# The steady phase of a decoder step: its blocks written out on four engines in place of a register loop

## What is computed

```python
def peer_ffn(x, w_q, sub_keys, peer_u, peer_v):
    q = (xt @ w_q).astype(jnp.float32).reshape(T, PEER_HEADS, 2, HALF)
    sc = jnp.einsum('thpd,hpnd->thpn', q, sub_keys.astype(jnp.float32))
    s_top, i_top = lax.top_k(sc, PEER_TOPK)
...
    def block(args):
        xc, ic, gc = args
        hu = jnp.einsum('tkd,td->tk', peer_u[ic], xc)
        act = jax.nn.gelu(hu, approximate=False) * gc
        return jnp.einsum('tk,tkd->td', act, peer_v[ic])

def decoder_layer(h, shift_prev, conv_buf, wkv, lp):
...
    h1 = layer_norm(ALPHA * h + mix, ln1_g, ln1_b)
    h2 = layer_norm(ALPHA * h1 + peer_ffn(h1, w_q, sub_keys, peer_u, peer_v), ln2_g, ln2_b)
```

## Time and profile before

| | |
|---|---|
| time, median of 3 runs | 3707.61 us (3704.52 to 3711.28) |
| the profiled execution's own time | 3712.13 us |
| its span, first to last instruction | 3710.4 us |
| PE busy with matmuls | 3241.3 us (87%) |
| DVE busy | 2429.9 us (65%) |
| POOL busy | 2110.3 us (57%) |
| ACT busy | 807.3 us (22%) |
| mean granted TensorE clock | 0.954 |
| moved by DMA | 1239.76 MB, 334 GB/s over the span |

### The profile page before, as it was taken

The page is one execution under the profiler, slowest core; times in us unless marked ns, Lnnn a source line. Parts: engine busy times, 40 slices in busy tenths (PEclk is TensorE's granted clock), DMA queues, the critical chain, the costliest instruction groups (busy, mean ns, idle before and its releaser), DMA issues.

```text
span 3710.4 us, 58003 instructions
## 1 busy us (share of the span) xinstructions
PE 3241.3 (87%) x17619; PEld 1712.6 (46%) x17619; DVE 2429.9 (65%) x5758; ACT 807.3 (22%) x1954; POOL 2110.3 (57%) x2172
## 2 busy tenths in 40 slices
PE   4996898599988998899889988998898899989877
PEld 3663565444544454445444544454445444533422
DVE  5463523757766776677667766776667767777695
ACT  2331001122222222222222222222222222222121
POOL 0012700466666666666666666666566666676575
PEclk9997999799999999999999999999999999999999
DMA  4344212899999999999999999999999999999997
GB/s 158 96 124 120 89 32 66 290 351 371 408 404 361 377 409 408 374 376 408 409 370 368 408 409 361 376 408 408 367 371 407 408 389 390 408 408 409 391 380 296
DMA packets 395689, 1239.76 MB, mean 334 GB/s; under 512 B 50834, under 2 KB 98326, under 8 KB 395216
## 3 DMA queue, kind: packets, MB, share of 16 engines
q0 software_dynamic: 302112, 1099.09, 76.6%
q1 hardware_dynamic: 91504, 134.41, 10.3%
q10 hardware_dynamic: 1728, 2.16, 0.2%
HBM read 1212.00 MB, written 31.94 MB: 335 GB/s over the span
## 4 chain that ended last, share of the span: by engine, by line
PE 53%; DMA 18%; DVE 10%; issue 7%; ACT 2%; POOL 2%; DVEq 0%; SPq 0%; ACTq 0%; POOLq 0%
PE ep_ps L1271 32%; DMA rings<-in_peer_v_dram,idx 15%; PE front_ps L1141 8%; PE ep_ps L1319 5%; PE front_ps L1193 3%; PE front_ps L1211 3%; DVE rings L1666 3%; DMA rings<-in_peer_u_dram,idx 2%; POOL rings L584 2%; ACT L1420 1%; ACT diag L1393 0%; DVE rings L1780 0%; PE front_ps L1202 0%; PE front_ps L1287 0%; PE front_ps L1220 0%
## 5 line engine op out<-in xcount | busy, mean ns | idle before, releaser
L1271 PE MATMUL ep_ps<-rings,diag 128*128 128x512 f32 x4096 | 2034.4, 625 | 288.4 <-ACT diag L1393 156.7
L584 POOL DMA_INDIRECT rings<-in_peer_u_dram,idx x1024 | 980.6, 958 | 777.2 <-issue 248.3
L1666 DVE CUSTOM_DVE_ANT_0 rings<-rings,x_ps 128x1024 f32<-128x1024 f32 x1024 | 1238.3, 1212 | 137.9 <-DMA rings<-in_peer_u_dram,idx 105.1
L584 POOL DMA_INDIRECT rings<-in_peer_v_dram,idx x1024 | 993.0, 970 | 470.6 <-issue 264.7
L1271 PEld LDWEIGHTS ep_ps<-rings,diag 128*128 128x128 f32 x4096 | 731.6, 195 | 1075.1 <-issue 772.5
L1393 ACT ACTIVATE diag<-ident,act_v 128x128 f32<-128x128 f32 x1024 | 347.7, 391 | 237.4 <-PE ep_ps L1271 141.6
L1211 PEld LDWEIGHTS front_ps<-h1T,wq_ring 128*128 128x128 f32 x2304 | 290.4, 199 | 63.5 <-issue 63.5
L1211 PE MATMUL front_ps<-h1T,wq_ring 128*128 128x128 f32 (+1 forms) x2304 | 290.7, 279 | 1.2 <-issue 1.2
L348 PE MATMUL job_ps<-rings,w_ring 128*128 128x352 f32 (+2 forms) x672 | 208.6, 473 | 7.7 <-ACTq L390 3.9
L1319 PE MATMUL ep_ps<-rings 128*128 128x352 f32 x576 | 197.1, 482 | 16.8 <-DVEq L1790 15.4
L1380 ACT ACTIVATE q_T<-front_ps 128x128 f32<-128x128 f32 (+1 forms) x144 | 38.5, 267 | 780.3 <-PE front_ps L1211 780.3
(11 more groups left out here) (349 smaller groups left out, 2877.5 us busy)
## 6 DMA issues: line engine op xcount, KB each, us to landing
wq_ring<-scratch_wq_tiles SPq DMA_DIRECT2D x144, 512.0 KB, 7.5
rings<-in_peer_u_dram,idx POOLq DMA_INDIRECT x1024, 13.7
rings<-in_peer_v_dram,idx POOLq DMA_INDIRECT x1024, 13.1
ops<-scratch_op_blocks SPq DMA_DIRECT2D x35, 256.0 KB, 8.7
scratch_wq_tiles<-in_w_q_dram SPq DMA_DIRECT2D x16, 512.0 KB, 5.1
w_ring<-in_w_in_dram SPq DMA_DIRECT2D x12, 512.0 KB, 3.9
rings<-in_w_in_dram SPq DMA_DIRECT2D x12, 512.0 KB, 3.9
xrow<-in_x_prompt_dram SPq DMA_DIRECT2D x8, 512.0 KB, 3.3
```

The lines of the kernel that those rows point to most:

```text
L584: return pool.indirect_dma_start(out=ring, out_offset=None, in_=table, in_offset=bass.IndirectOffsetOnAxis(ap=index, axis=0))
L1271: mm = pe.matmul(out_ps[:, half, :], diag[:, s % RING, :], v[:, s % RING, half * 512:(half + 1) * 512], start=head == 0 and s == 0, stop=h ...
L1666: dve.tensor_tensor_reduce(u[:, s % RING, :], u[:, s % RING, :], x, 1.0, 0.0, ALU.mult, ALU.add, hu[:, par, s:s + 1]).then_inc(dots, 1)
```

## The change

In `over_turns` the `Fori` of six bodies and the body written out behind it become one Python loop over seven bodies, unrolled when the program is built. All turn numbers are plain integers then. The order of the work on each engine stays the same. The loop of SP is not touched.

```diff
             a_turn(0, 0, None, sums=False)
             a_turn(1, 1, 1)
-            with eng.Fori(0, TBLOCKS - 2) as b:
+            for b in range(TBLOCKS - 1):
                 rest_of_block(b, b * H, b + 1)
                 start_of_block(b + 1, b * H + H, b + 2)
-            b = TBLOCKS - 2
-            rest_of_block(b, b * H, b + 1)
-            start_of_block(b + 1, b * H + H, b + 2)
-            rest_of_block(b + 1, b * H + H, b + 2)
+            rest_of_block(TBLOCKS - 1, (TBLOCKS - 1) * H, TBLOCKS)
             a_turn(TBLOCKS * H, 0, None, dots_left=False)
             finish(TBLOCKS - 1)
```

## The result

| | before | changed | |
|---|---|---|---|
| median | 3706.35 us (3704.52 to 3711.28, 4 runs) | 3643.43 us (3640.84 to 3645.71, 4 runs) | ratio 0.9828, 95% interval 0.9811 to 0.9845 |
| profiled execution | 3712.13 us | 3640.84 us | |
| its span, granted clock | 3710.4 us, 0.954 | 3638.6 us, 0.965 | |

The change takes 62.9 us off, 1.7%. The forecast was 53 us off, 3655 us: the direction, the place and nearly the size of the main term were right, and 10 us were missing. The stated range, 3640 to 3670 us, holds the result; the forecast's own narrower one, 3649 to 3660 and 3 us on either side, does not.

A forecast was written before the change was run, and what follows sets the result against it. A body was taken as bound partly by PE (turn 2) and partly by the DMA; jumps 51 us plus registers 2 us make 53 off 3707.6, giving 3655 us, range 3640 to 3670 us.

The forecast's parts named there:

- The jumps back: Turn 2 after each of five jumps on PE, ACT, DVE, POOL: removing the stands gives 51 us, bounds 47.3 to 54.7.
- given back behind the jumps: Rest of the five later bodies: turns behind a stand run ahead, so up to 5.4 us was already made up.
- Nearer to nothing because a turn that the DMA holds gives none of it: Register instructions in the loop bodies: removing them gives 2 us, between nothing and 4.3, most turns being held by the DMA.
- one bare place on ACT: ACT between gate and first diagonal: 0.39 us with a register instruction, 0.30 without; over all turns at most 4.3 us.
- The twin of turn 2 and turn 3: Looped against written-out turns 2 and 3: each gives 0.4 us without register instructions.
- Turn 6: 48.64 us looped, 44.75 written out: no evidence for registers, as the DMA sets both and carries 1.6 MB less written out.
- The rival of the registers: Turns 0 and 1: sequencer load sets the pace there too, 18 us more gain, 3637 us; chance 0.09.
- The DMA hides the stands: Turns 3 to 7: freed time returns as waits for v, 3707 us, or 3681 if half hidden; chance 0.08 together.
- Written-out code stands too: Seven written-out bodies: never-reused code makes engines stand at each new stretch, 71 us against 51 saved, 3726 us; chance 0.03.
- The cost of a jump goes with the length of what is jumped over: SP's loop, kept: its jump costs little, 0.7 us, its body having 76 instructions against ACT's 412.
- The signs named ahead: If right: no ACT or DVE issue waits after turn 1, turn 2 at 40.5 to 41.5 us, rest of body 321 to 325.

The follow-up runs named there:

- regs_all: Against the kernel before: bodies written out on all four engines, block number kept in a register, so no jump and all register instructions; 3661.72 us.
- regs_act: The change, but ACT alone keeps the block number in a register, the other three engines having plain numbers; 3643.91 us.
- regs_pe: The change, but PE alone keeps the block number in a register, the other three engines having plain numbers; 3641.33 us.
- two_bodies: Against the kernel before: loop of three trips with two bodies written out in each, two jumps back in place of five; 3681.42 us.
- sp_straight: The change, with SP's loop written out too; 3643.38 us.

## Why the prediction was right, and where it was short

- **The jumps back**, forecast 51 us: 46.4 measured by taking them alone (before against regs_all). Right in mechanism and place; the measured value is 9% smaller and 1 us under the lower bound of 47.3, and its interval (41.5 to 53.8) holds the forecast. In the profiles, turn 2 of blocks 1 to 5 takes 258.2 us before, 210.1 in regs_all and 206.6 in the change. The part that was to be given back behind the jumps cannot be told from the spread of the medians; it stays open. What was not seen is that PE and POOL stand at the jump as well (5.9 and 4.7 us), hidden behind ACT; it did not matter to a change that takes the jump off all four.
- **"Nearer to nothing because a turn that the DMA holds gives none of it"**: this is the step that failed. The registers were put at 2 us with an upper bound of 4.3, and took 18.3 (16.3 by the ratios). Two things were wrong in it. The bound came from one bare place on ACT, whose registers cost nothing (regs_act), while DVE's, which were named as the largest count, were given no row of their own; DVE cost 15.0 us. And a turn at 409 GB/s is not held for good: its length is what is left to move, divided by 409. Turn 7 gave 10.4 us in six bodies, the most of all but turn 2, and had 0.8 MB a body less to move, while turns 3, 1 and 4, in which the DMA engines had room, took more. (Turn 3's share is what turn 2 no longer moves during a stand.) The prediction also put PE's register instructions at 215 a body, while PE's instructions differ by 118 in all, and by 117 on the pages of regs_pe and the change; it has no weight, since they cost nothing.
- **Two errors of opposite sign.** The jumps took 4.6 us less than forecast and the registers 16 us more; the total is off by 10 us because part of the second was covered by the first. That the result still lies in 3640 to 3670 is in part luck.
- **The twin of turn 2 and turn 3** (0.4 us between looped and written out) was a sound reading of those turns and a poor sample of the body: turns 2 and 3 differ by little, 7 and 1 by 1 to 1.7 us. Turn 6 was rightly thrown out as evidence; it gave 0.9 us in six bodies.
- **The rival of the registers** (3637 us, chance 0.09) was nearest in kind: 18 us more was its price and 16 us more was the truth. It placed them in turns 0 and 1, which gave 4.8 us together; and the time, 3643.4, came out above 3637 mostly because the jumps were 4.6 us less.
- **The DMA hides the stands**: refuted in the form it had, since the freed time stayed free. But its arithmetic was right. A body moves 145 MB in both kernels, 355 us at 408.5 GB/s; before it took 373, now 361.6. By this estimate some 6 us a body are left until the DMA sets it all.
- **Written-out code stands too**: refuted. No wait for "issue" of ACT's diagonals or DVE's dots is left in the six bodies, though each is now code that is run once. The Trainium skill (Runtime: NRT & Kernel Launch, Instruction fetch mechanics) says that straight code is fetched ahead; these runs agree, with no such wait in the six bodies.
- **"The cost of a jump goes with the length of what is jumped over"**: not borne out among the long bodies. ACT, with 412 instructions, stands longer than DVE with 1235 and PE with 1302, and two_bodies, with twice the length, pays no more for a jump. That SP's jump costs nothing held (sp_straight); whether its 76 instructions are the reason was not tried.
- **The signs named ahead**: turn 2 at 40.5 to 41.5 us with a clock of 1.00 came true in three of five blocks; the others show 42.27 at 0.96. The rest of a body, forecast at 321 to 325 us, took 318.6 to 322.0, four of six below it. Turns 0 and 1 by over 1 us each, the sign of the registers rival: turn 1 by 1.0, turn 0 by nothing.

## What to carry to other kernels

Where several engines run one long loop body and work hand over hand, cut the trace at a repeated instruction and compare the stretch behind the jump with its twin without one. The difference is near the price of the jump (51 us by the twins, 46.4 by a run of its own), and what shows is the longest stand, with the other engines' stands hidden behind it. So the jump has to go on all of them, or be announced on all, before all of it is gained.

Where a transfer engine is near full on the average, ask for every small saving whether it lets an earlier turn with room take bytes from a later one that is full: a bound by bytes in one turn is no proof that nothing upstream of it counts.

Register arithmetic cost nothing on three engines here and 15 us on the fourth, and a bare wait of 0.09 us before a critical instruction stood on one of those where it was free. So test it engine by engine: neither the longest bare wait nor the engine's idle time says where it counts.

## What the runs showed of the hardware

**At a plain jump back over this body ACT stands 8.7 to 9.8 us, PE 5.9 (2.8 without a jump), DVE 5.6 and POOL 4.4 to 5.0**, and DVE 0.6 when it is announced; SP, with 76 instructions in its body, shows no such cost. Why ACT's is 3 us longer than the others' was not tried.

**Turn 2 has two lengths with the same work.** In the changed kernel it alternates between 40.7 us at a granted clock of 1.00 and 42.3 us at 0.96, with the same stand of PE ahead of it. In the longer ones the clock falls during the first matmuls. Four take 2.85 us (timeline), and the granted clock is 0.65 over the next 3.5 us, before it is 1.00 again (windows, of the same block):

```profile
2229.61 2.85 PE L1268 MATMUL ep_ps<-rings,diag 128*128 128x512 f32 x4 [2.81 <-ACT diag L1390]
```

```profile
2228.55:2231.50 2.95, 1.89 (x4) 0.82 (x4) 2.70 (x5) 1.20 (x4) 1.76 (x3) 0.84 1.02 405
2231.50:2235.00 3.50, 3.50 (x21) 1.81 (x20) 1.62 (x5) 0.67 (x2) 1.84 (x3) 0.65 1.03 410
2235.00:2240.00 5.00, 5.00 (x41) 2.44 (x40) 1.16 (x4) 2.94 (x7) 2.35 (x3) 1.00 1.02 409
```

The same four take 1.96 us in the timeline of the shorter turn above, and 3.78 at 1.2 GHz behind a jump. In two of three such blocks nothing of it is lost: turn 3 then takes 44.3 us and not 45.95, and both turns together 86.6 us either way. In these the 1.6 us that the turn is longer by are made up in the next; in the kernel before, behind a jump, the turn was 10 us longer and the next one gave back 1.6 us at most.

**Registers on PE, ACT and POOL cost nothing that shows**: the three medians lie 2.1 us below to 0.5 us above the change's, where each ratio's interval is some 5 us wide on either side. By the pages' counts they and their waits are 117, 188 and 193 instructions a body. DVE's, 348 a body, cost 15 us in six bodies.
